# The mixer's level products as two column tiles of 64 stationary columns

## The reference, cut to what matters

```python
diff = b[:, :, :, None, :] - b[:, :, None, :, :]
decay = jnp.where(causal[:, :, None], jnp.exp(jnp.minimum(diff, 0.0)), 0.0)
a = jnp.einsum('bhtk,bhtsk,bhsk->bhts', qc, decay, kc)
o_intra = jnp.einsum('bhts,bhsv->bhtv', a, vc)
```

## Time and profile before

| | us |
|---|---|
| median of 3 runs | 1328.69 |
| lowest, highest | 1326.96, 1329.12 |
| span of the profiled execution | 1325.9 |
| TensorE busy in it | 1279.8 (97%) |
| VectorE busy | 605.0 (46%) |
| ScalarE busy | 403.8 (30%) |
| GpSimd busy | 370.3 (28%) |

### The profile page before, as it was taken

The page is one execution under the profiler, slowest core; times in us unless marked ns, Lnnn a source line. Parts: engine busy times, 40 slices in busy tenths (PEclk is TensorE's granted clock), DMA queues, the critical chain, the costliest instruction groups (busy, mean ns, idle before and its releaser), DMA issues. The chain is left out here.

```text
span 1325.9 us, 18663 instructions
## 1 busy us (share of the span) xinstructions
PE 1279.8 (97%) x6804; PEld 805.8 (61%) x6804; DVE 605.0 (46%) x1027; ACT 403.8 (30%) x987; POOL 370.3 (28%) x417
## 2 busy tenths in 40 slices
PE   6999999999989999999999999999999999999995
PEld 5788889798979898894455455333333333333342
DVE  4224878687868787752122214521122122122225
ACT  4023636354444546252110123111111111111113
POOL 2256655556464746120100000810000000000002
PEclk9999999999999999998999999899999999999999
DMA  7793212122121222513226534499999999999996
GB/s 224 241 340 91 80 41 72 53 61 64 49 65 49 78 66 64 151 41 120 75 69 249 206 127 151 174 409 419 426 424 424 427 426 428 424 425 425 425 424 260
DMA packets 130854, 290.63 MB, mean 219 GB/s; under 512 B 6420, under 2 KB 109049, under 8 KB 112733
## 3 DMA queue, kind: packets, MB, share of 16 engines
q1 hardware_dynamic: 125168, 277.89, 55.2%
q0 software_dynamic: 3552, 8.20, 1.6%
q10 hardware_dynamic: 2061, 3.50, 0.8%
HBM read 269.32 MB, written 24.12 MB: 221 GB/s over the span
## 5 line engine op out<-in xcount | busy, mean ns | idle before, releaser
L2064 DVE TENSOR_SCALAR ee<-ee 128x256 f32<-128x256 f32 x32 | 9.8, 307 | 336.0 <-ACT ee L1951 336.0
L2043 POOL DMA_INDIRECT expert_out<-yy,row_at x30 | 29.4, 980 | 391.5 <-ACT yy L1937 391.5
L710 PE MATMUL bank<-h_sums,ring 128*128 128x256 f32 x384 | 91.1, 380 | 0.0
L710 PEld LDWEIGHTS bank<-h_sums,ring 128*128 128x128 f32 x384 | 72.0, 190 | 9.1
L710 PE MATMUL bank<-h_mix,weights_0lo 128*128 128x256 f32 x256 | 61.7, 396 | 8.2 <-issue 6.8
L1742 PE MATMUL bank<-x_rows,select 128*64 128x512 bf16 x416 | 62.9, 382 | 0.0
L710 PEld LDWEIGHTS bank<-h_mix,weights_0lo 128*128 128x128 f32 x256 | 50.0, 199 | 18.6 <-issue 11.9
L1338 PE MATMUL bank<-x_rows,ring 128*128 128x512 f32 x128 | 58.1, 618 | 3.1 <-PEq L470 3.1
L710 PE MATMUL bank<-h_sums,weights_0hi 128*128 128x256 f32 x256 | 60.5, 379 | 0.0
L720 PE MATMUL bank<-weights_0lo,h_mix 128*128 128x128 f32 x512 | 58.9, 276 | 0.0
L1338 PE MATMUL bank<-weights_2down,ring 128*128 128x512 f32 x128 | 57.1, 598 | 1.7 <-DVE weights_2down L1540 1.7
(11 more groups left out here) (382 smaller groups left out, 2601.3 us busy)
## 6 DMA issues: line engine op xcount, KB each, us to landing
weights_0lo<-in_w_gate_up SPq DMA_DIRECT2D x11, 2048.0 KB, 17.2
weights_0hi<-in_w_gate_up SPq DMA_DIRECT2D x11, 2048.0 KB, 21.6
weights_0down<-in_w_down SPq DMA_DIRECT2D x11, 2048.0 KB, 21.4
weights_1down<-in_w_down SPq DMA_DIRECT2D x11, 2048.0 KB
weights_1lo<-in_w_gate_up SPq DMA_DIRECT2D x11, 2048.0 KB, 18.0
weights_1hi<-in_w_gate_up SPq DMA_DIRECT2D x11, 2048.0 KB, 22.4
weights_2lo<-in_w_gate_up SPq DMA_DIRECT2D x10, 2048.0 KB, 17.6
ring<-in_w_gate_up SPq DMA_DIRECT2D x10, 2048.0 KB, 22.0
```

Of the source, the lines that this page charges most:

```text
L710: mm = pe.matmul(bank[:, 0:HALF_T], w[:, k], h[:, k], start=(fresh and k == 0), stop=(k == HALF_K - 1), skip_group_check=True)
L2043: pool.indirect_dma_start(out=half_rows, out_offset=bass.IndirectOffsetOnAxis(ap=row_at[:, e:e + 1], axis=0), in_=yy[e % 2][:], in_offset= ...
L2064: st.link(dve.tensor_scalar(ee[q][:], ee[q][:], BIG, 1.0, ALU.min, ALU.add))
```

## The change

The product of a level is made in two halves. Keys 0 to 63 and keys 64 to 127 of a chunk can only be in the same block with queries of their own half, from level 1 on. So for each chunk and each half u a matmul has the 64 columns of that half as stationary operand and its own 32 query columns as moving one, and writes to PSUM partitions 64u to 64u+63: column tile u of the array. At level 0 only keys 0 to 63 and queries 64 to 127 are wanted: one matmul per chunk, 64 by 64, in column tile 0. A level from 1 on now has half the columns in PSUM. The masks and `tmp` become half as wide, the masked products handle half as many elements, and each add becomes two of 64 partitions. `gh` gets a tile of its own. ScalarE copies the same elements from other places.

```diff
-        level_mask = sb("level_mask", [P, LEVELS, 64], ctx=front_scope)
+        level_mask = sb("level_mask", [P, LEVELS, 32], ctx=front_scope)
...
-            for l in range(LEVELS):
+            for l in range(1, LEVELS):
 
                 h = 64 >> l
-                lm = g["level_mask"][:, l].rearrange("p (b i) -> p b i", i=h)
-                st.did(pool.affine_select(out=lm, in_=lm, compare_op=ALU.is_ge, fill=0.0, base=0,
-                                          pattern=[[-2 * h, 64 // h], [0, h]], channel_multiplier=1))
...
+                for u in range(2):
+                    lm = g["level_mask"][u * 64:(u + 1) * 64, l].rearrange("p (b i) -> p b i", i=h)
+                    st.did(pool.affine_select(out=lm, in_=lm, compare_op=ALU.is_ge, fill=0.0, base=0,
+                                              pattern=[[-2 * h, 32 // h], [0, h]], channel_multiplier=1))
...
-            tmp = sb("tmp", [P, 2, NT, 64], c=inner)
+            tmp = sb("tmp", [P, 2, NT, 32], c=inner)
+            gate_exp = sb("gate_exp", [P, SEQ], c=inner)
...
-            gh = tmp[:].rearrange("p l c t -> p (l c t)")
+            gh = gate_exp[:]
...
                     for c in range(NT):
-                        rv = rr[l % 4][:, c * P:(c + 1) * P].rearrange("p (b h) -> p b h", h=2 * h)[:, :, h:2 * h]
-                        mm = pe.matmul(bank[:, c0 + c * 64:c0 + c * 64 + 64], rr[l % 4][:, c * P:(c + 1) * P], rv,
-                                       start=True, stop=True)
+                        if l == 0:
+                            at = c * P
+                            mm = pe.matmul(bank[0:64, c0 + c * 64:c0 + (c + 1) * 64], rr[0][:, at:at + 64],
+                                           rr[0][:, at + 64:at + P], start=True, stop=True)
+                            continue
+                        for u in range(2):
+                            own = rr[l % 4][:, c * P + u * 64:c * P + (u + 1) * 64]
+                            rv = own.rearrange("p (b h) -> p b h", h=2 * h)[:, :, h:2 * h]
+                            mm = pe.matmul(bank[u * 64:(u + 1) * 64, c0 + c * 32:c0 + (c + 1) * 32], own, rv,
+                                           start=True, stop=True)
                     mm.then_inc(lev, 1)
...
+                    own = bank[:, 0:n * 256].rearrange("p (l x) -> p l x", l=n)[:, :, 0:NT * 32]
                     mst_.link(dve.tensor_tensor(
-                        tmp[:, 0:n], bank[:, 0:n * 256].rearrange("p (l c t) -> p l c t", l=n, t=64),
-                        g["level_mask"][:, l:l + n].unsqueeze(2).broadcast_to([P, n, NT, 64]), ALU.mult))
+                        tmp[:, 0:n], own.rearrange("p l (c t) -> p l c t", t=32),
+                        g["level_mask"][:, l:l + n].unsqueeze(2).broadcast_to([P, n, NT, 32]), ALU.mult))
...
-                        av = aa[:].rearrange("p c (b i) -> p c b i", i=2 * h)[:, :, :, h:2 * h]
                         if i > l:
                             dve.wait_ge(acc, 7 * m + i)
-                        dve.tensor_tensor(av, av, tmp[:, i - l].rearrange("p c (b i) -> p c b i", i=h),
-                                          ALU.add).then_inc(acc, 1)
+                        for u in range(2):
+                            rows = slice(u * 64, (u + 1) * 64)
+                            av = aa[rows, :, rows].rearrange("p c (b i) -> p c b i", i=2 * h)[:, :, :, h:2 * h]
+                            last = dve.tensor_tensor(av, av, tmp[rows, i - l].rearrange("p c (b i) -> p c b i", i=h),
+                                                     ALU.add)
+                        last.then_inc(acc, 1)
```

More of the change, by code:

```diff
@@ L308, in _ @@
                              channel_multiplier=0, allow_small_or_imprecise_dtypes=True))
-            for l in range(LEVELS):
+            for l in range(1, LEVELS):
                 h = 64 >> l
-                lm = g["level_mask"][:, l].rearrange("p (b i) -> p b i", i=h)
-                st.did(pool.affine_select(out=lm, in_=lm, compare_op=ALU.is_ge, fill=0.0, base=0,
-                                          pattern=[[-2 * h, 64 // h], [0, h]], channel_multiplier=1))
-                st.sync()
-                st.did(pool.affine_select(out=lm, in_=lm, compare_op=ALU.is_ge, fill=0.0, base=h - 1,
-                                          pattern=[[2 * h, 64 // h], [0, h]], channel_multiplier=-1))
+                for u in range(2):
+                    lm = g["level_mask"][u * 64:(u + 1) * 64, l].rearrange("p (b i) -> p b i", i=h)
+                    st.did(pool.affine_select(out=lm, in_=lm, compare_op=ALU.is_ge, fill=0.0, base=0,
+                                              pattern=[[-2 * h, 32 // h], [0, h]], channel_multiplier=1))
+                    st.sync()
+                    st.did(pool.affine_select(out=lm, in_=lm, compare_op=ALU.is_ge, fill=0.0, base=h - 1,
+                                              pattern=[[2 * h, 32 // h], [0, h]], channel_multiplier=-1))
+            st.sync()
             quarter = token_quarters(h_mix)
@@ L1029, in levels_out @@
                     act.wait_ge(ke_r, 2 * m + 1)
-                    first, second = (AL0[:, n * 256:(n + 1) * 256].rearrange("p (c t) -> p c t", t=64) for n in range(2))
+                    first = AL0[:, 0:256].rearrange("p (c t) -> p c t", t=64)
+                    second = AL0[:, 256:384].rearrange("p (c t) -> p c t", t=32)
                     act.activation(aa[0:64, :, 64:128], first[0:64], ACT.Copy).then_inc(acc, 1)
-                    act.activation(aa[0:32, :, 32:64], second[0:32, :, 0:32], ACT.Copy)
-                    act.activation(aa[64:96, :, 96:128], second[64:96, :, 32:64], ACT.Copy).then_inc(acc, 1)
+                    act.activation(aa[0:32, :, 32:64], second[0:32], ACT.Copy)
+                    act.activation(aa[64:96, :, 96:128], second[64:96], ACT.Copy).then_inc(acc, 1)
                 def normed(m, mp):
```

## The result

The changed kernel takes 1334.96 us (median of 9 runs, 1331.98 to 1335.93) against 1328.13 us (9 runs beside it). The ratio is 1.0048, 95% interval 1.0035 to 1.0062: **slower by 6.4 us** by that ratio (the medians are 6.8 apart), where 9.7 us faster was forecast. The profiled execution's span is 1330.5 us against 1325.9.

What follows compares the result with a forecast made beforehand. TensorE was taken to set the pace, VectorE next. TensorE's 2.06 us a head, limited by VectorE's last add in six heads, summed to 9.7 us: 1328.7 to 1319.0 us, range 1315 to 1324.

Steps and rivals of the forecast that it cites:

- Products: TensorE's level products in the mixer: 53 steps of 0.109 us become 53 of 0.055, saving 2.86 us a head.
- Switches: TensorE changing between full array and column tiles: 0.27 us a group, 0.80 us a head lost for three groups.
- Masks and the adds' own price: VectorE: masked products save 0.67 us; five adds become pairs of 0.625 us each, costing 0.83 more.
- VectorE's last add comes 0.16 us later: VectorE's chain of masked products and adds into aa: net delay of its end by 0.16 us.
- The sum, head by head: Mixer gains: heads 1, 3, 5 0.39 us each; 0, 2, 4 1.48; 6 and 7 2.06; in all 9.7.
- the feed-bound one: Rival: TensorE's couples no faster than L852's instructions, 0.055 us a matmul; 5.5 us lost, 1334.2 us; chance 0.13.
- VectorE eats the gain: Rival: 64-partition adds cost what full ones do, 0.43 instead of 0.29 us; together nothing gained, 1328.5 us; chance 0.08.

Runs made afterwards that it cites:

- e2: Kernel before with the column tiles alone; masks, masked products and full-height adds as before: 1318.91 us, ratio 0.9928.
- e8: Changed kernel with the masked product written back in place in PSUM instead of tmp, no wait added: 1320.4 us, ratio 0.9932.
- e5: e2 plus GpSimd waiting for VectorE's last add into aa before its weight sums of the next turn: 1319.99 us, ratio 0.993 to the kernel before.
- e6: e5 with GpSimd waiting for the last add already before its last two joins of the turn: 1322.18 us, ratio 0.9951 to the kernel before.
- e9: e2 with the masked product in place in PSUM, full-height adds, no wait added: 1321.0 us, ratio 0.9934 to the kernel before.
- e12: Control: kernel before with the masked product in place in PSUM, no tiles: 1328.58 us, ratio 1.0003.
- e3: Kernel before with only the adds split, each into two of 64 partitions: 1329.58 us, ratio 1.0006.

## Why the prediction was wrong, step by step

**Products: right.** 0.055 us a couple was forecast, 0.058 is measured. Level 0, in one tile, runs at 0.058 a matmul too.

**Switches: right.** The first tile comes 0.20 us after the last full-array matmul (0.20 forecast), the next full-array one 0.15 after the last tile (0.12 forecast). In head 6, where little holds it up, TensorE reaches the aa sum 1.96 us sooner and in head 7 2.04; 2.06 was the forecast.

**Masks and the adds' own price: right.** 0.42 and 0.29 for the masks; a pair of adds takes 0.285+0.290 without overlap, 0.62 with its wait, forecast 0.625.

**The step that failed** is "VectorE's last add comes 0.16 us later", and with it "The sum, head by head". It took the durations of VectorE's operations as fixed, and moved TensorE alone. But GpSimd's sums follow TensorE too, and the forecast speedup itself moved them from 49.5 to 48.2 us behind the scores, onto adds that then ended at 48.6. The trace of before had the sign: in head 1 a pair of adds took 1.29 us instead of 0.88, because a join ran beside the second. That row lies in the part left out of the earlier trace rows shows another, head 2's last add at 0.60 instead of 0.43. I took both for constants. The measured last add comes 3.8 us later in heads 1, 3 and 5 and 1.45 us later in 0, 2 and 4. The split of the adds is what makes the collision dear. With the tiles alone (e2) the sums start as early, and the last add ends 0.2 us sooner than before in heads 0, 2 and 4 and only 1.5 to 1.6 us later in 1, 3 and 5. The split makes the chain 0.16 us longer by its own price, and gives two operations in place of one that can each be caught: level 6 takes 0.98 and 1.26 us, where e2's single add took 1.06, and behind level 5's second add, caught for 1.38, everything comes later.

With the collisions gone and everything else as in the change (e8), the gain is 8.8 us against the runs beside it, 9.7 forecast. **The rivals:** the feed-bound one gives nearly the measured time, 1334.2, by a mechanism that is not there; its price was right by chance. "VectorE eats the gain" was the right engine with the wrong reason (a full price for half-height adds) and too small a size. That a neighbour's work moves with TensorE's had no rival of its own, and so the range missed.

**Left open:** why e5, e6 and e9, in which heads 1, 3 and 5 wait less than in e2, are not faster than it. The traces say where the time is. From head 0's scores to head 7's, e5 and e6 are in fact 0.9 and 1.6 us shorter than e2 (426.9 and 426.2 against 427.8). From head 7's aa sum to the experts' first gathering product (L1742 in the kernel before), a stretch in which none of these kernels differ, e5, e6 and e9 take 313.2 to 313.5 us, e2 and e8 310.3. In e9 the mixer is 0.7 us longer: behind heads 1 and 3, from the aa sum to the next scores, it takes 18.3 and 18.5 us at granted clocks of 0.81 and 0.81, e2 15.1 and 17.7 us at 0.89 and 0.81. The clock of whole runs points the same way. Within one kernel a lower mean granted clock goes with a longer time, about 0.73 us for each 0.001 over the runs on record. By an estimate from this, put at one clock of 0.990, e2, e5, e6, e8 and e9 lie between 1320.0 and 1320.8 us. So the differences between these five are mostly of the clock, and the shorter waits in heads 1 and 3 bring no gain that can be told from nothing. I made no run that holds the clock and the branch fixed. By their medians the five are 7 to 10 us below the kernel before, and e2, e5, e8 and e9 can't be told apart.

## What to carry to other kernels

A speedup of the bounding engine moves everything that its semaphores release. List for each engine what starts earlier, and check which operations that someone waits for will then run beside it; here 1 us lay between the adds (48.5) and the sums (49.5), less than the 2 us by which TensorE was made faster. In this case many short operations were caught more dearly than few long ones: with the same tiles the collisions cost nothing that can be measured with full-height adds (e2 against e9), and 14.6 us with split ones (the change against e8). When VectorE and GpSimd must overlap, keep one operand of VectorE's tensor-by-tensor operations in PSUM: in e8 that was worth 14.6 us and cost nothing (e12). And a part that is free alone (e3) together with one that gains alone (e2) can still lose.

## What the runs showed of the hardware

In the changed kernel, an add of VectorE with both operands in SBUF that began while an operation of GpSimd was running ended 0.14 to 0.15 us after it: so did all 20 adds that lasted over 0.5 us (0.28 us became 0.70 to 1.38). Four adds that met only the last 0.1 us of it were not held. The full-height adds of the kernel before and of e2 ended 0.28 to 0.29 us after it. An add that began first kept its length, and GpSimd's operation was the longer one (a join of 0.95 us instead of 0.73). With one operand in PSUM the adds kept their 0.28 to 0.29 us (e8). A TENSOR_SCALAR from SBUF to SBUF (L1141) took 1.28 to 1.35 us beside the sums instead of 0.43, while the masked product from PSUM kept its 0.29. Two column tiles of 64 stationary and 32 moving fp32 columns take 0.058 us a couple, weight loads included.
